# Mixture-of-experts stage: one sorted list of choices, windows copied by POOL, expert outputs through DRAM

## The reference, cut to what matters

```
scores = sigmoid(h @ w_router)                 # 256 tokens x 16 experts
sel = scores + b_router                        # best group of 4 experts, then its best 2
combine = one_hot(idx) * wts                   # two weights for each token, sum 1
for e in range(16):
    y_e = (silu(h @ w1[e]) * (h @ w3[e])) @ w2[e]      # 1024 -> 512 -> 1024
    y = y + combine[:, e:e+1] * y_e
out = rmsnorm(x + g2 * y, final_g)
```

## Time and profile before

| what | value |
|---|---|
| median of 3 runs | 1164.57 us (1162.86 to 1167.72) |
| profiled execution, its time | 1157.83 us |
| its span | 1156.1 us |
| PE busy | 974.9 us (84%) |
| DVE busy | 661.8 us (57%) |
| ACT busy | 553.1 us (48%) |
| POOL busy | 129.1 us (11%) |

### The profile page before, as it was taken

The page is one execution under the profiler, slowest core; times in us unless marked ns, Lnnn a source line. Parts: engine busy times, 40 slices in busy tenths (PEclk is TensorE's granted clock), DMA queues, the critical chain, the costliest instruction groups (busy, mean ns, idle before and its releaser), DMA issues.

```text
span 1156.1 us, 15025 instructions
## 1 busy us (share of the span) xinstructions
PE 974.9 (84%) x5944; PEld 831.9 (72%) x5946; DVE 661.8 (57%) x875; ACT 553.1 (48%) x884; POOL 129.1 (11%) x282
## 2 busy tenths in 40 slices
PE   3898879987898788986689797478999999999993
PEld 1588758876787668876677696466778787787872
DVE  1475664447643565434644474634786677677773
ACT  2455543245333543236322252435776676677661
POOL 3003310125001250021500100000000000000000
PEclk9899899998999989999899988569999999999997
DMA  8455575324843337435465239406787788877850
GB/s 306 142 181 145 131 192 144 83 56 119 222 115 87 100 94 204 115 114 157 114 186 182 92 110 349 143 2 218 254 303 275 259 291 277 298 246 275 313 209 38
DMA packets 215860, 206.38 MB, mean 179 GB/s; under 512 B 32817, under 2 KB 154330, under 8 KB 215146
## 3 DMA queue, kind: packets, MB, share of 16 engines
q1 hardware_dynamic: 215785, 205.38, 56.0%
HBM read 192.74 MB, written 12.62 MB: 178 GB/s over the span
## 4 chain that ended last, share of the span: by engine, by line
PE 63%; DVE 12%; DMA 7%; ACT 7%; POOL 4%; issue 4%; SPq 2%; DVEq 0%; POOLq 0%; ACTq 0%
PE bank L2145 60%; DVE w_lo L1902 5%; PE bank L2148 3%; SPq L494 2%; DMA lane<-inverse 2%; DMA raw<-in_w_ada_dram 2%; ACT w_hi L1287 2%; POOL lane L824 2%; POOL lane L826 1%; DMA half_raw<-in_w_in_dram 1%; DMA problem_rows<-lane 1%; DVE y_lo L2002 1%; DMA lane<-problem_rows 1%; DVE half_lo L1488 1%; ACT half_hi L898 1%
## 5 line engine op out<-in xcount | busy, mean ns | idle before, releaser
L1902 DVE TENSOR_TENSOR w_lo<-raw,w_hi 128x2048 fp32r<-128x2048 f32 x96 | 219.0, 2287 | 107.1 <-ACT w_hi L1287 106.4
L2145 PE MATMUL bank<-hT,half_hi 128*128 128x256 f32 (+1 forms) x1024 | 235.2, 326 | 17.1 <-ACT staged L996 13.6
L1287 ACT CAST w_hi<-raw 128x2048 fp32r<-128x2048 f32 x96 | 183.0, 1909 | 95.3 <-PE bank L2145 95.3
L2145 PEld LDWEIGHTS bank<-hT,half_hi 128*128 128x128 f32 x1024 | 173.8, 199 | 33.7 <-ACT staged L996 14.6
L1488 DVE TENSOR_TENSOR half_lo<-half_raw,half_hi 128x1024 fp32r<-128x1024 f32 x88 | 108.4, 1234 | 111.6 <-ACT half_hi L898 111.4
L2145 PE MATMUL bank<-w_hi,hT 128*128 128x512 f32 x512 | 168.9, 399 | 0.7 <-ACT hT L1310 0.7
L2145 PE MATMUL bank<-hT,half_lo 128*128 128x256 f32 (+1 forms) x512 | 163.0, 318 | 0.0
L2145 PE MATMUL bank<-lane 128*128 128x128 f32 (+1 forms) x1072 | 140.3, 290 | 22.2 <-DMA lane<-inverse 10.9
L2145 PEld LDWEIGHTS bank<-lane 128*128 128x128 f32 (+1 forms) x1072 | 128.7, 198 | 34.0 <-issue 16.8
L2145 PEld LDWEIGHTS bank<-w_hi,hT 128*128 128x128 f32 x512 | 97.0, 190 | 21.8 <-ACT hT L1310 0.9
L898 ACT CAST half_hi<-half_raw 128x1024 fp32r<-128x1024 f32 x88 | 92.4, 1052 | 40.6 <-PE bank L2145 21.8
(11 more groups left out here) (273 smaller groups left out, 1518.8 us busy)
## 6 DMA issues: line engine op xcount, KB each, us to landing
raw<-in_w_e_dram SPq DMA_DIRECT2D x96, 1024.0 KB, 5.3
half_raw<-in_w_in_dram SPq DMA_DIRECT2D x64, 512.0 KB, 4.3
half_raw<-in_w_ada_dram SPq DMA_DIRECT2D x32, 512.0 KB, 4.0
raw<-in_w_ada_dram SPq DMA_DIRECT2D x8, 1024.0 KB, 9.4
dense<-staged SPq DMA_DIRECT2D x32, 128.0 KB, 2.9
lane<-inverse SPq DMA_DIRECT2D x16, 256.0 KB, 5.3
lane<-inverse_turned SPq DMA_DIRECT2D x16, 256.0 KB, 5.5
half_raw<-in_w_proj_a_dram SPq DMA_DIRECT2D x8, 512.0 KB, 4.2
```

What stands on the lines that cost most here:

```text
L1287: act.copy(e_hi[n % WBUF][:, :], raw[n % RING][:, :]).then_inc(s["hi_ready"], 1)
L1902: dve.tensor_tensor(e_lo[n % WBUF][:, :], raw[n % RING][:, :], e_hi[n % WBUF][:, :].bitcast(F32), ALU.subtract)\
L2145: return nc.tensor.matmul(dst, lhsT, rhs, start=start, stop=stop)
```

## The change

The 512 choices (two for each token) are put into one list sorted by expert. One gather at the start brings all 512 columns into `hT`; an expert's tokens are then 128 neighbouring columns of it, from `first_int[q]` on. The first expert reads them in place; for the others POOL copies the window (128 partitions x 2048 numbers, both halves) to one of two buffers `window`. Per-pair picks, gathers, transposes, weights, `y_high`/`y_low` and scatters are gone, as are the zero matmuls. ACT copies the output of an expert to `y_out`, and SP sends it to DRAM (`y_dram`, 512 KiB) in between the loads. At the end POOL fetches each token's two rows by indirect DMA, and DVE weighs and adds them. The PSUM banks freed make two sets of 4 (`work_bank`).

```diff
+        y_out = [sb(f"y_out{g}", [P, D]) for g in range(2)]
+        y_tok = nc.alloc_sbuf_tensor_at("y_tok", [P, 2, 2, D], F32, offset=LANE_AT)
+        window = [nc.alloc_sbuf_tensor_at(f"window{g}", [P, 2, KC, P], F32R, offset=LANE_AT + 8 * D * g) for g in range(2)]
...
 SP
+            def store_rows(q):
+                sp.wait_ge(s["y_copied"], 2 * q + 2)
+                sp.dma_start(y_dram[q * P:(q + 1) * P, :], y_out[q % 2][:, :]).then_inc(y_stored[q % 2], 16)
             for n, (v, q, half_) in enumerate(STREAM):
+                if n >= 22 and (n - 22) % 6 == 0:
+                    store_rows((n - 22) // 6)
...
+            for q in range((len(STREAM) - 23) // 6 + 1, EXPERTS - 1):
+                store_rows(q)
+            for nh in range(2):
+                sp.wait_ge(s["y_copied"], 2 * (EXPERTS - 1) + nh + 1)
+                sp.dma_start(y_dram[last_rows, nh * N:nh * N + N], y_out[1][:, nh * N:nh * N + N]).then_inc(s["stored"], 16)
...
+            for t in range(2):
+                sp.wait_ge(s["out_ready"], t + 1)
+                sp.dma_start(out[0, t * P:(t + 1) * P, :], x_lat[:, t, :]).then_inc(s["stored"], 16)
 POOL
+            def token_rows(n, t, late, experts):
+                at = bass.IndirectOffsetOnAxis(ap=row_int[:, late, 2 * n + t:2 * n + t + 1], axis=0)
+                return pool.indirect_dma_start(out=y_tok[:, n, t, :], out_offset=None, in_=y_dram[0:experts * P, :], in_offset=at)
+            def take_window(q):
+                if q >= 3:
+                    pool.wait_ge(s["unit_used"], UP_FIRST[q - 2] + 4)
+                at = pool.value_load(first_int[0:1, 0, q:q + 1], min_val=0, max_val=LAST_WINDOW)
+                pool.tensor_copy(window[q % 2][:, :, :, :], hT[:, :, :, bass.ds(at, P)].bitcast(F32))
...
+            take_window(1)
+            take_window(2)
+            for q in range(3, EXPERTS):
+                take_window(q)
+            pool.wait_ge(s["rows_placed"], 1)
+            pool.wait_ge(y_stored[0], 16 * (EXPERTS // 2))
+            pool.wait_ge(y_stored[1], 16 * (EXPERTS // 2 - 1))
+            for t in range(2):
+                token_rows(0, t, 0, EXPERTS - 1).then_inc(s["first_rows"], 16)
+            pool.wait_ge(s["stored"], 32)
+            for t in range(2):
+                token_rows(1, t, 0, EXPERTS).then_inc(second_rows[t], 16)
 ACT
+            def gather_copy(c):
+                act.wait_ge(s["gathered"], 2 * c + 1)
+                act.copy(hT_hi[:, c, :], bank[gather_bank(c, 0)][:, :]).then_inc(s["turned_hi"], 1)
-            def y_high(q, nh):
+            def y_copy(q, nh):
                 act.wait_ge(s["unit_used"], DOWN_FIRST[q] + nh + 1)
+                if q >= 2 and nh == 0:
+                    act.wait_ge(y_stored[q % 2], 16 * (q // 2))
+                act.copy(y_out[q % 2][:, nh * N:nh * N + N], work_bank(q, 2 + nh)[:, :]).then_inc(s["y_copied"], 1)
 DVE
+            for t in range(2):
+                own.mark(dve.tensor_scalar(pick[:, t, :], slot_iota[:, :], pair_at[:, 0, t:t + 1], None, ALU.is_equal))
+            for t in range(2):
+                dve.scalar_tensor_tensor(out=pick[:, t, :], in0=slot_iota[:, :], scalar=pair_at[:, 1, t:t + 1],
+                                         in1=pick[:, t, :].bitcast(F32), op0=ALU.is_equal, op1=ALU.add)
...
+            for c in range(KC):
+                dve.wait_ge(s["gathered"], 2 * c + 2)
+                dve.tensor_copy(hT_lo[:, c, :], bank[gather_bank(c, 1)][:, :]).then_inc(s["turned_lo"], 1)
+            ... 21 small instructions: each token's two rows in y_dram (row_int) and weights (pair_weight)
             for q in range(EXPERTS):
+                for n in ahead[:3]:
+                    expert_low(n)
                 act_product(q)
+                for n in ahead[3:]:
+                    expert_low(n)
                 act_low(q)
...
+            def weigh(n, t):
+                return dve.scalar_tensor_tensor(out=y_tok[:, n, t, :], in0=y_tok[:, n, t, :], scalar=pair_weight[:, n, t:t + 1],
+                                                in1=ada_vec[:, 3, :], op0=ALU.mult, op1=ALU.mult)
+            own.mark(weigh(0, 0))
+            own.after(weigh(0, 1))
+            own.mark(dve.tensor_tensor(x_lat, x_lat, y_tok[:, 0, :, :], ALU.add))
+            for t in range(2):
+                dve.wait_ge(second_rows[t], 16)
+                own.after(weigh(1, t))
+                dve.tensor_tensor(x_lat[:, t, :], x_lat[:, t, :], y_tok[:, 1, t, :], ALU.add).then_inc(s["x2_ready"], 1)
 PE
+            pe.wait_ge(s["picks_ready"], 2)
+            for c in range(KC):
+                for half, src in ((0, h2_hi), (1, h2_lo)):
+                    if c >= 4:
+                        pe.wait_ge(s["turned_lo" if half else "turned_hi"], 4 + c - 3)
+                    for t in range(2):
+                        ins = mm(bank[gather_bank(c, half)][:, :], src[:, t, c * P:(c + 1) * P], pick[:, t, :], t == 0, t == 1)
...
             for q in range(EXPERTS):
+                up_half(q, 0)
+                up_half(q, 1)
                 if q:
+                    down_half(q - 1, 0)
+                    down_half(q - 1, 1)
                 turn_act(q)
+            down_half(EXPERTS - 1, 0)
+            down_half(EXPERTS - 1, 1)
```

More of the change, by code:

```diff
@@ L470, in block_kernel, with gather_bank, work_bank @@
         DOWN_FIRST = [6 * q + 8 for q in range(EXPERTS - 1)] + [6 * EXPERTS - 2]
[L471 to L475, removed]
+        assert len(STREAM) == ALL_UNITS
+        def gather_bank(c, half):
+            return (2 * c + half) % 8
+        def work_bank(q, n):
+            return bank[4 * (q % 2) + n]
         def four(t):
@@ L865, in _ @@
             o_norm(PAIRS - 1)
-            for at, squared, power in ((0, "x1_squared", "x1_power"), (2, "x2_squared", "x2_power")):
-                pool.wait_ge(s[squared], 1)
-                own.after(pool.tensor_scalar(x_stat[:, 1, at:at + 2], x_stat[:, 0, at:at + 2], 1.0 / D, EPS,
+            pool.wait_ge(s["x1_squared"], 1)
+            own.after(pool.tensor_scalar(x_stat[:, 1, 0:2], x_stat[:, 0, 0:2], 1.0 / D, EPS, ALU.mult, ALU.add))
+            pool.tensor_tensor(x_stat[:, 2, 0:2], x_stat[:, 1, 0:2], half_neg[:, 0:2], ALU.pow).then_inc(s["x1_power"], 1)
@@ L1353, in _ @@
-                for n in ahead[3:5]:
+                for n in ahead[2:5]:
                     expert_high(n)
                 if q:
-                    y_high(q - 1, 0)
+                    y_copy(q - 1, 0)
                 for n in ahead[5:]:
@@ L1930, in _ @@
             expert_low(3)
+            own.mark(dve.memset(both[:, 1, 0:1], 0.0))
             dve.wait_ge(s["logits_exp"], 1)
@@ new lines, in _ @@
+            own.after(dve.tensor_scalar(first_of[:, 3, :], first_of[:, 3, :], float(EXPERTS * P), None, ALU.add))
+            own.mark(dve.tensor_tensor(row_of[:, 0, :, :], row_of[:, 0, :, :], first_of[:, 3, :].unsqueeze(1)
+                                       .to_broadcast([P, 2, EXPERTS]), ALU.mult))
+            own.after(dve.tensor_tensor(row_of[:, 1, :, :], place[:, :, :], first_of[:, 1, :].unsqueeze(1)
+                                        .to_broadcast([P, 2, EXPERTS]), ALU.add))
@@ new lines, in _ @@
+            own.mark(dve.tensor_tensor(row_of[:, 2, :, :], choice[:, :, :], second_of, ALU.mult))
+            own.mark(dve.tensor_scalar(row_int[:, 1, :], row_sum[:, :, :].rearrange("p n t -> p (n t)"),
+                                       -(P * EXPERTS // N + 1.0), None, ALU.add))
+            for n in range(2):
+                own.mark(dve.tensor_scalar(row_int[:, 0, 2 * n:2 * n + 2], row_sum[:, n, :], -(P * EXPERTS // N + 1.0),
+                                           (EXPERTS - 1 + n) * P - 1.0, ALU.add, ALU.min))
@@ L1990, in act_product @@
+            own.settle()
+            dve.tensor_reduce(pair_weight[:, :, :], row_of[:, 1:3, :, :], AX, ALU.add).then_inc(s["rows_placed"], 1)
             def act_product(q):
@@ L2019, in _ @@
                 act_product(q)
-                for n in ahead[3:5]:
+                for n in ahead[3:]:
                     expert_low(n)
-                if q:
-                    y_low(q - 1, 0)
-                for n in ahead[5:]:
-                    expert_low(n)
-                if q:
-                    y_low(q - 1, 1)
-                act_low(q)
-                if not even and g + 1 < GATHERS:
-                    picks(g + 1)
-            for nh in range(2):
-                y_low(EXPERTS - 1, nh)
@@ L2678, in up_half @@
+            def up_half(q, m):
+                dst = work_bank(q, m)[:, :]
+                ours = window[q % 2][:, :, :, :] if q else hT[:, :, :, 0:P]
+                if q and m == 0:
+                    pe.wait_ge(s["window_ready"], q)
+                if q >= 2 and m == 0:
+                    pe.wait_ge(s["act_split"], q - 1)
                 for kh in range(2):
```

620 lines of the change are left out of this document (195 added, 425 removed).

## The result

| | median, us | lowest and highest | profiled execution, us | span, us |
|---|---|---|---|---|
| before | 1166.14 | 1162.86 to 1168.40 | 1157.8 | 1156.1 |
| after | 1090.31 | 1086.48 to 1092.34 | 1089.1 | 1087.3 |

The ratio is 0.935, with a 95% interval of 0.931 to 0.939: 76 us off, where 63 were forecast (1103 us).

What follows compares the result with a forecast made beforehand. It took PE to bound the kernel. Gains of 58.9 (stream), 3.4 (first expert) and 2.0 (tail), less 2.8 (routing), took 61.5 us off 1157.8: 1096.3 profiled, 1103 as a median, range 1084 to 1128.

Steps and rivals of the forecast that it cites:

- PE's part: Expert stage: with scatter, gather and stalls gone, an expert keeps 72 matmuls and one turn, 17.05 us of PE.
- DVE with POOL is the new bound: Expert stage: splits wait for whole window copies, so DVE needs 18.1 us an expert, over PE's 17.05; chance 0.52.
- C: Time of POOL's window copy of 2048 numbers for an expert: taken as 3.7 us, between 1.7 and 4.9.
- the exclusion: Expert stage: a DVE split and a POOL copy wait for each other to finish; act_product, reading a bank, is exempt.
- DMA's step: Expert stage: 6.82 MB an expert at 405 GB/s takes 16.8 us; later landings make some splits wait, adding 0.3 us.
- P: Time of one expert in the stream: forecast 18.4 us, from DVE's 18.1 plus 0.3 for late loads.
- A: Rival, expert stage: PE stays the bound, copy under 2.6 us or in DVE's idle time; 17.1 an expert, 1086; chance 0.20.
- B: Rival, expert stage: DMA becomes the bound at 350 GB/s, 19.5 us an expert, 1122 us in all; chance 0.17.
- Routing: From the choice to up(0): 16.7 us after the change for 13.9 before, a loss of 2.8.
- First expert: From up(0) to up(1): 18 us for 21.4, a gain of 3.4, with DVE's placing against two window copies.
- Stream: From up(1) to the end of down(15): 281.3 us for 340.2, a gain of 58.9.
- Tail: From the end of down(15) to the span's end: 20.3 us for 22.3, a gain of 2.0.

Runs made afterwards that it cites:

- ring5: A fifth buffer for the experts' weight units, against the changed kernel's four, with act_hi laid over an earlier tile: 1078.9 us, ratio 0.929.
- the control: The changed kernel run once more, unaltered, on the chip of the three kernels beside it: 1094.5 us, ratio 0.941.

## Why the forecast was right, and where it was not

**PE's part** was right. 17.05 us an expert was worked out, and 17.14 to 17.16 was seen wherever the loads were in time.

**The step that failed is "DVE with POOL is the new bound".** Its price C was put at 3.7 by the POOL copy of 256 numbers; the copy of 2048 takes 1.9, near the memset's slope (1.7), the low end of the bounds. From 0.611 us at 256 numbers to 1.896 at 2048 are 0.72 ns a number, an estimate from these two rows; by it 0.43 us of the small row were its fixed part, where the forecast had taken 0.13 to 0.2. The longest split was 3.4 us, where the sign of being right was 5 to 6. What the forecast read of the exclusion itself was right, and so was its exception: `act_product` took 0.68 us beside two running copies (at 799.81 and 816.89). Here the Trainium skill's GPSIMD Engine Reference, section "Engine selection", was right: its "roughly line-rate" had made an estimate of 1.9.

**DMA's step had the right shape and the wrong quantity.** It asked whether the rate suffices (6.82 MB at 405 GB/s, 16.8 us) and added 0.3 us for loads that land later. The rate does suffice: ring5 is the proof. What falls short is time ahead. A buffer goes round in landing + 1.91 + 2.31 and a little for the steps between, 4.4 in all, and four of them at (7.5 + 4.4) / 4 allow a unit each 2.98 us, 17.9 an expert. In the kernel before the same rule with its landing of 5.3 gives 9.7 / 4 x 6 = 14.6, far under the 22.67 of then, so it could not be seen. The forecast named "a load is issued at the end of a split four units before", and compared it with 5.3 us; a sum round the whole ring with a longer landing stood one line away.

So P came out at 17.9 to 18.0 where 18.4 was forecast, between the rivals A (17.1) and B (19.5), by a cause that is neither. A's condition (a copy under 2.6) was met, and PE was still not the bound. B named the right queue, and its sign came in (splits wait for ACT, ACT for landings of over 7 us), but its 350 GB/s is not a ceiling: ring5 moved 386 GB/s, loads and stores together, over 206 us. Nor do the 19.0 us an expert hold that the forecast worked out from the 358 GB/s of the Trainium skill's DMA: Bandwidth & Descriptors, "Specifications": ring5 took 17.16.

**The terms.** Routing: 17.0 for 16.7. First expert: 15.1 for 18, nearly all from C, since two copies stand there against DVE's placing. Two of its instructions on short rows, `L2008` and `L2010`, took 1.83 and 1.88 us as they met those copies. Stream: 277.7 for 281.3, with 1.9 of it the clock in down(15), which no step had. Tail: 22.4 for 20.3. Store and landing were 3.7 for 3.1, the first fetch 6.0 for 4.5, of which the descriptors beside DVE's addition are 1.55; the second fetch was hidden, but DVE then weighed and added two halves in turn, 5.0 us where 1.3, 1.28 and 1.15 were put down; square, power and scaling were 4.1 for 3.2, and the last store with its issue 3.0 for 3.5; the 1.6 put down for the rest lies in these.

From 1103 to 1090.3 are thus: 3.2 ahead of the change, 2.9 first expert, 3.6 stream, less 0.3 and 2.1, and 5.5 because the forecast lifted its sum by 6.7 to a median, and the profiled execution of after was only 1.2 under its own. Two errors of the bound (C too large, the ring not seen) had opposite signs, and that the number came out so near is in part luck.

## What to carry to other kernels

When an edit takes time off the bound, work out a period for each ring of buffers: (issue to landing + every step until the buffer is free) / buffers, with a landing longer than today's (here 7.5 us for 5.3); a rate that suffices doesn't make a ring deep enough. A DMA share of 1.0 and PE at 97% can both stand beside a chain that is neither's, so go by who waits for whom, and take away bytes and add a buffer before you call it bandwidth. A price scaled up from a far smaller row belongs at the end of a range, not in the middle.

## What the runs showed that was not expected

- POOL's making of descriptors for an indirect fetch (0.94 us) is held up by a DVE addition of two tensors in SBUF that is already running: in nine executions a fetch that started during the addition ended 0.81 to 0.82 us after it. A fetch that started 0.11 to 0.12 us ahead of the addition took 0.94 beside it, in three executions.
- TensorE's granted clock fell in some executions and not in others after a pause of 2.05 to 2.14 us ahead of down(15): 0.60 to 0.77 in five of eight, 1.00 in three. After a pause of 1.45 us it was 1.00 in all three. Ahead of the first turn, after 3.2 to 3.45 us, it fell in six of 11.
- Taking 448 KB an expert off the stores left the time and the landings (7.2 for 7.5 us) nearly as they were. What of a landing of 7.5 us is queueing and what is the pieces' own was not settled: with pieces four times as large it was 7.2 for all weights, and 7.8 where only w1 and w3 had them, against 7.6 in the control.
